# First attention of an fp32 two-block model: another order for heads 0-3 and heads 4-7 around the projection blocks

## What is computed

```python
def probs(qb, k):
    s = jnp.einsum("bhqd,bhkd->bhqk", qb, k).astype(jnp.float32) * scale + bias
    return jax.nn.softmax(jnp.where(causal, s, -jnp.inf), axis=-1)
a = probs(qb1, k1) - lam * probs(qb2, k2)
out = jnp.einsum("bhqk,bhkv->bhqv", a.astype(v.dtype), v)
...
of = of * lax.rsqrt(jnp.mean(jnp.square(of), -1, keepdims=True) + LN_EPS) * subln_g
of = of * (1.0 - lambda_init)
return of.reshape(bsz, seq, V_WIDTH) @ w_o
```

## Time and profile before

| | us |
|---|---|
| median of three runs (1342.65 to 2119.0) | 1343.82 |
| profiled execution | 1342.31 |
| its span, first to last instruction | 1340.6 |

### The profile page before, as it was taken

How to read it: one execution, slowest core, us unless ns; L and a number is a source line. 1 busy time by engine, 2 the same in 40 slices (tenths; PEclk the granted TensorE clock), 3 DMA queues, 4 the chain that set the end, 5 groups by cost and what they waited for, 6 DMA issues and landing times.

```text
span 1340.6 us, 15674 instructions
## 1 busy us (share of the span) xinstructions
PE 1248.6 (93%) x6428; PEld 858.3 (64%) x6428; DVE 622.3 (46%) x944; ACT 451.7 (34%) x698; POOL 199.0 (15%) x174
## 2 busy tenths in 40 slices
PE   7998989999988996889999998989999898899998
PEld 7986654444537884654444536879887546778776
DVE  3996422221216565522221216594489644444544
ACT  3596311111113455311111113465466213444432
POOL 5000300000000000200000000185788130000000
PEclk9999989999999997989999998999999899999999
DMA  9800959999994530589999992533344133363450
GB/s 336 295 0 10 413 240 428 427 427 428 428 393 162 189 126 0 226 332 429 427 427 429 426 384 98 186 126 126 126 159 156 63 126 128 126 237 138 180 196 32
DMA packets 68162, 321.22 MB, mean 240 GB/s; under 512 B 4072, under 2 KB 12661, under 8 KB 55419
## 3 DMA queue, kind: packets, MB, share of 16 engines
q1 hardware_dynamic: 64944, 308.57, 58.1%
q0 software_dynamic: 2592, 11.42, 2.4%
q10 hardware_dynamic: 554, 0.23, 0.1%
HBM read 317.02 MB, written 3.18 MB: 239 GB/s over the span
## 4 chain that ended last, share of the span: by engine, by line
PE 75%; DVE 15%; ACT 4%; issue 3%; POOL 2%; DMA 0%; DVEq 0%; ACTq 0%; POOLq 0%
PE bank L1477 29%; PE bank L1638 25%; PE bank L1630 5%; PE bank L1542 3%; PE bank L2090 3%; PE bank L1680 2%; DVE w_lo L646 2%; ACT w_hi L934 1%; DVE arena L2217 1%; POOL w_lo L646 1%; POOL xtok L870 1%; DVE rows L2731 1%; DVE arena L2750 1%; PE bank L1761 1%; POOL xtok L868 1%
## 5 line engine op out<-in xcount | busy, mean ns | idle before, releaser
L934 ACT ACTIVATE w_hi<-ring 128x2048 fp32r<-128x2048 f32 (+1 forms) x96 | 180.1, 1880 | 213.8 <-PE bank L1477 208.2
L646 DVE TENSOR_TENSOR w_lo<-ring,w_hi 128x2048 fp32r<-128x2048 f32 (+1 forms) x70 | 156.6, 2240 | 182.6 <-ACT w_hi L934 182.1
L646 POOL TENSOR_TENSOR w_lo<-ring,w_hi 128x512 fp32r<-128x512 f32 x104 | 152.0, 1494 | 84.9 <-ACT w_hi L934 84.9
L1477 PE MATMUL bank<-w_hi,x_hi 128*128 128x512 f32 (+1 forms) x432 | 121.7, 401 | 18.0 <-ACT arena L1397 6.5
L1477 PE MATMUL bank<-w_lo,x_hi 128*128 128x512 f32 (+1 forms) x432 | 118.8, 395 | 3.7 <-POOL w_lo L646 3.4
L1477 PE MATMUL bank<-w_hi,x_lo 128*128 128x512 f32 (+1 forms) x432 | 118.3, 394 | 0.0
L1638 PE MATMUL bank<-ring,moe_x 128*64 128x512 f32 x384 | 113.0, 594 | 1.5 <-issue 1.5
L1638 PE MATMUL bank<-arena,moe_x 128*64 128x512 f32 x384 | 112.9, 594 | 0.0
L1477 PEld LDWEIGHTS bank<-w_hi,x_hi 128*128 128x128 f32 x432 | 79.5, 194 | 36.4 <-issue 11.8
L1477 PEld LDWEIGHTS bank<-w_lo,x_hi 128*128 128x128 f32 x432 | 81.8, 194 | 23.3 <-POOL w_lo L646 6.4
L2390 DVE TENSOR_TENSOR y_r<-bank,y_r 128x512 fp32r<-128x512 f32 x32 | 22.1, 692 | 158.7 <-ACT y_r L934 158.7
(11 more groups left out here) (330 smaller groups left out, 1863.1 us busy)
## 6 DMA issues: line engine op xcount, KB each, us to landing
ring<-in_w_in_dram SPq DMA_DIRECT2D x15, 2048.0 KB, 8.0
ring<-in_moe_w_gate_dram SPq DMA_DIRECT2D x12, 2048.0 KB, 16.3
arena<-in_moe_w_down_dram SPq DMA_DIRECT2D x12, 2048.0 KB, 20.6
arena<-in_moe_w_gate_dram SPq DMA_DIRECT2D x12, 2048.0 KB, 15.9
ring<-in_moe_w_down_dram SPq DMA_DIRECT2D x12, 2048.0 KB, 18.0
ring<-in_moe_w_up_dram SPq DMA_DIRECT2D x12, 2048.0 KB, 16.1
arena<-in_moe_w_up_dram SPq DMA_DIRECT2D x12, 2048.0 KB, 19.2
wslots<-in_moe_w_up_dram SPq DMA_DIRECT2D x8, 2048.0 KB, 20.6
```

The lines of the kernel that those rows point to most:

```text
L646: last = ops.tensor_tensor(part(w_lo, label, hb)[:, x].bitcast(F32R), ring_half(label, hb)[:, x], part(w_hi, label, hb)[:, x], ALU.subtract)
L934: return s.activation(dst, src, ACT.Copy)
L1477: last = mm(bank(use_)[:, at:at + cols], still, moving, start=start and opens and (hb, n, k) == (0, 0, 0), stop=stop and closes and (hb, n ...
```

## The change

- Heads 0-3: all of their units (0 to 7) now lie inside v0, k1 and q1, two steps to a unit; their norm, transposes and split lie inside v1. The split result goes to a buffer of its own, `o_hi` and `o_lo` (`o_r`, at 14336 of the arena), since `x_hi` and `x_lo` are still read by v1.
- Heads 4-7: units 8 to 11 begin inside v1, the rest inside wo0 and wo1. The lone stretch between v1 and wo0 is gone; a short one (two calls) is between wo0 and wo1.
- The last unit's sum (15) goes into a bank of its own (`o15`, bank 6) and is scaled by its own instruction (`last_head_out`), so that the other three heads can be scaled earlier.
- In the lists of ScalarE and VectorE, `weights(u)` is no longer tied to `weights_T(u - 2)`, and `logits` and `difference` are written out singly.

The diff, indentation cut; left out are changes of signatures and calls that follow from the new buffer.

```diff
@@ -131,6 +131,9 @@
+O_AT = 7 * KD * T
+with nc.sbuf_tensor("below_o", [P, O_AT], F32), nc.sbuf_tensor("o_r", [P, 2, 4, T], F32) as o_r:
+    pass
...
     use(("pT", u), 6)
     if h % 4 == 0:
         use(("o", qt, h // 4), 7)
+use("o15", 6)
 for b in range(4):
     use(("oT", b), (0, 1, 4, 5)[b])
...
-def head_squares(qt, g):
+def head_squares(qt, g, heads):
     freed(act, ("o", qt, g))
-    for h in range(4):
...
@@ -1203,50 +1208,66 @@
 keys_out("k", kT, 0)
 highs(("v", 0))
 keys_out("q", qT, 0)
+weights(0)
 high(("k", 1), 0)
-weights(0)
 weights(1)
+weights_T(0)
+values_out(0)
 high(("k", 1), 1)
-values_out(0)
-weights_T(0)
 weights_T(1)
+weights(2)
+weights(3)
+weights_T(2)
 high(("q", 1), 0)
-weights_T(2)
+weights(4)
+weights_T(3)
+weights(5)
+weights_T(4)
+high(("q", 1), 1)
+weights_T(5)
 keys_out("k", kT, 1)
-high(("q", 1), 1)
-weights_T(3)
-weights_T(4)
-head_squares(0, 0)
+weights(6)
+head_squares(0, 0, range(4))
+weights(7)
+weights_T(6)
 high(("v", 1), 0)
-weights_T(5)
+weights_T(7)
+high(("v", 1), 1)
 keys_out("q", qT, 1)
-high(("v", 1), 1)
-weights_T(6)
-weights_T(7)
+head_squares(1, 0, range(4))
+head_roots(0)
+weights(8)
+weights(9)
+values_out(1)
+for b in range(2):
+    heads_high(b, o_hi, slice(2 * b, 2 * b + 2), slice(0, T))
 weights_T(8)
-head_squares(1, 0)
-head_roots(0)
-values_out(1)
+weights(10)
 high(("wo", 0), 0)
 weights_T(9)
+weights(11)
+weights_T(10)
 high(("wo", 0), 1)
-weights_T(10)
-for b in range(2):
-    heads_high(b, slice(2 * b, 2 * b + 2), slice(0, T))
 weights_T(11)
+weights(12)
+weights(13)
+head_squares(0, 1, range(4))
 weights_T(12)
+high(("wo", 1), 0)
+weights(14)
 weights_T(13)
+weights(15)
 root_ahead()
-head_squares(0, 1)
 tile_root(0)
 weights_T(14)
-high(("wo", 1), 0)
+high(("wo", 1), 1)
+heads_high(2, x_hi, slice(4, 8), slice(0, P))
 weights_T(15)
-heads_high(2, slice(4, 8), slice(0, P))
-high(("wo", 1), 1)
-head_squares(1, 1)
+head_squares(1, 1, range(3))
+freed(act, "o15")
+head_squares(1, 1, (3,))
 tile_root(1)
-heads_high(3, slice(4, 8), slice(P, T))
+heads_high(3, x_hi, slice(4, 8), slice(P, T))
 root_ahead()
@@ -1772,14 +1793,16 @@
 def weighted(u):
     qt, h = units[u]
-    o = ("o", qt, h // 4)
-    if h % 4 == 0:
+    o, at = ("o", qt, h // 4), h % 4 * VD
+    if u == len(units) - 1:
+        o, at = "o15", 0
+    if h % 4 == 0 or o == "o15":
         claim(pe, o)
     freed(pe, ("pT", u))
     for kt in range(qt + 1):
-        last = mm(bank(o)[:, h % 4 * VD:(h % 4 + 1) * VD], diffT[:, u % 2, kt, :],
+        last = mm(bank(o)[:, at:at + VD], diffT[:, u % 2, kt, :],
                   vtok[:, kt, h * VD:(h + 1) * VD], start=kt == 0, stop=kt == qt)
-    if h % 4 == 3:
...
@@ -1799,6 +1822,8 @@
         scores(0)
     elif (hb, t) == (1, 0):
         scores(1)
+    elif (hb, t) == (1, 1):
+        weights_T(0)
 keys("k", 0, arrives="ln1")
 keys("q", 0)
@@ -1806,55 +1831,43 @@
 def during_k(hb, n):
     if (hb, n) == (0, 0):
         scores(2)
-        weights_T(0)
     elif (hb, n) == (0, 1):
         evacuated(("v", 0))
         weighted(0)
+        weights_T(1)
+    elif (hb, n) == (0, 2):
+        scores(3)
+        weighted(1)
     elif (hb, n) == (0, 3):
-        scores(3)
-        weights_T(1)
+        weights_T(2)
     elif (hb, n) == (1, 0):
-        weighted(1)
+        scores(4)
+        weighted(2)
     elif (hb, n) == (1, 1):
-        scores(4)
-        weights_T(2)
+        weights_T(3)
     elif (hb, n) == (1, 2):
-        weighted(2)
+        scores(5)
+        weighted(3)
+    elif (hb, n) == (1, 3):
+        weights_T(4)
 def during_q(hb, n):
     if (hb, n) == (0, 0):
-        scores(5)
-        weights_T(3)
+        scores(6)
+        weighted(4)
     elif (hb, n) == (0, 1):
-        weighted(3)
+        weights_T(5)
+    elif (hb, n) == (0, 2):
+        scores(7)
+        weighted(5)
     elif (hb, n) == (0, 3):
-        scores(6)
-        weights_T(4)
+        weights_T(6)
     elif (hb, n) == (1, 0):
-        weighted(4)
+        weighted(6)
     elif (hb, n) == (1, 1):
-        scores(7)
-        weights_T(5)
+        weights_T(7)
     elif (hb, n) == (1, 2):
-        weighted(5)
-def during_v(hb, t):
-    if (t, hb) == (0, 0):
-        weights_T(6)
-    elif (t, hb) == (0, 1):
-        weighted(6)
-        evacuated(("k", 1), ("q", 1))
-        scores(8)
-    elif (t, hb) == (1, 0):
-        scores(9)
-        weights_T(7)
-    elif (t, hb) == (1, 1):
         weighted(7)
-        scores(10)
-        weights_T(8)
-keys("k", 1, steps=during_k)
-keys("q", 1, steps=during_q)
-linear_tok(("v", 1), ("v", 1), steps=during_v, order=[(hb, t) for t in range(NT) for hb in range(2)])
 def heads_T(b, chunks, ts):
-def unit(u):
-    if u + 2 < len(units):
-        scores(u + 2)
-    weights_T(u)
-def out_heads(g, **more):
+def during_v(hb, t):
+    if (t, hb) == (0, 1):
+        evacuated(("k", 1), ("q", 1))
+        scores(8)
+        scores(9)
+    elif (t, hb) == (1, 0):
+        pe.wait_ge(sem("onorm"), NT)
+        for b in range(2):
+            heads_T(b, (2 * b, 2 * b + 1), range(NT))
+        scores(10)
+        weights_T(8)
+    elif (t, hb) == (1, 1):
+        freed(pe, ("v", 1, 0))
+        weighted(8)
+        weights_T(9)
+        scores(11)
+keys("k", 1, steps=during_k)
+keys("q", 1, steps=during_q)
+linear_tok(("v", 1), ("v", 1), steps=during_v, order=[(hb, t) for t in range(NT) for hb in range(2)])
+def out_heads(g, xh, xl, **more):
     split_product(("wo", g), [(("wo", t, h), HALF, slice(t * P, (t + 1) * P), slice(h * HALF, (h + 1) * HALF))
                               for t in range(NT) for h in range(2)],
-                  True, x_hi[:, 4 * g:4 * g + 4, :], x_lo[:, 4 * g:4 * g + 4, :], start=not g, stop=bool(g),
-                  **more)
+                  True, xh, xl, start=not g, stop=bool(g), **more)
 def during_wo(hb, n):
     if (hb, n) == (0, 0):
+        weights_T(10)
+        weighted(9)
         for b in range(2):
             freed(pe, ("oT", b))
     elif (hb, n) == (0, 1):
+        weighted(10)
+        weights_T(11)
+        scores(12)
+    elif (hb, n) == (0, 2):
+        freed(pe, ("v", 1, 1))
         weighted(11)
-        unit(12)
-    elif (hb, n) == (0, 2):
+        scores(13)
+    elif (hb, n) == (1, 0):
+        weights_T(12)
+        scores(14)
+    elif (hb, n) == (1, 1):
         weighted(12)
-        unit(13)
-    elif (hb, n) == (0, 3):
+        weights_T(13)
+        scores(15)
+    elif (hb, n) == (1, 2):
         weighted(13)
-        unit(14)
-    elif (hb, n) == (1, 0):
-        weighted(14)
-        unit(15)
-    elif (hb, n) == (1, 1):
-        pe.wait_ge(sem("onorm"), NT + 1)
-        heads_T(2, range(4, 8), (0,))
-        weighted(15)
+    elif (hb, n) == (1, 3):
+        weights_T(14)
 def during_wo1(hb, n):
     if (n, hb) == (0, 0):
         freed(pe, ("oT", 2))
+    elif (n, hb) == (1, 0):
+        weights_T(15)
+    elif (n, hb) == (0, 1):
+        weighted(15)
     elif (n, hb) == (2, 0):
         pe.wait_ge(sem("onorm"), 2 * NT)
         heads_T(3, range(4, 8), (1,))
         freed(pe, ("oT", 3))
-freed(pe, ("v", 1, 0))
-weighted(8)
-unit(9)
-weighted(9)
-unit(10)
-freed(pe, ("v", 1, 1))
-pe.wait_ge(sem("onorm"), NT)
-for b in range(2):
-    heads_T(b, (2 * b, 2 * b + 1), range(NT))
-weighted(10)
-unit(11)
-out_heads(0, steps=during_wo)
-out_heads(1, steps=during_wo1, order=[(hb, 2 * t + h) for t in range(NT) for hb in range(2) for h in range(2)])
+out_heads(0, o_hi, o_lo, steps=during_wo)
+pe.wait_ge(sem("onorm"), NT + 1)
+heads_T(2, range(4, 8), (0,))
+weighted(14)
+out_heads(1, x_hi[:, 4:8, :], x_lo[:, 4:8, :], steps=during_wo1, order=[(hb, 2 * t + h) for t in range(NT) for hb in range(2) for h in range(2)])
 norm_T("ln2", before=2)
 experts(1)
...
-def pair_of(u):
-    if u + 1 < len(units):
-        logits(u + 1)
-    difference(u)
-def heads_out(qt, g):
+def heads_out(qt, g, n=4):
     ready(dve, ("o", qt, g))
-    heads = lambda x: x.rearrange("p (h d) -> p h d", h=4)
+    heads = lambda x: x.rearrange("p (h d) -> p h d", h=n)
     u0 = 8 * g + 4 * qt
-    free(v.tensor_tensor(heads(otok[:, qt, g * HALF:(g + 1) * HALF]), heads(bank(("o", qt, g))[:]),
-                         bcast(dinv[:, 0, u0:u0 + 4].unsqueeze(2), 4, VD), ALU.mult), ("o", qt, g))
+    free(v.tensor_tensor(heads(otok[:, qt, g * HALF:g * HALF + n * VD]), heads(bank(("o", qt, g))[:, 0:n * VD]),
+                         bcast(dinv[:, 0, u0:u0 + n].unsqueeze(2), n, VD), ALU.mult), ("o", qt, g))
+def last_head_out():
+    ready(dve, "o15")
+    free(v.tensor_scalar(otok[:, 1, 7 * VD:8 * VD], bank("o15")[:, 0:VD], dinv[:, 0, 15:16], None, ALU.mult),
+         "o15")
 def heads_norm(g, ts, root):
     dve.wait_ge(sem("ostd"), root)
@@ -2540,49 +2568,63 @@
 low(dve, v, ("v", 0), 1)
 dve.wait_ge(sem("bias1"), 16)
 logits(0)
+difference(0)
+logits(1)
 low(dve, v, ("k", 1), 0)
-logits(1)
-difference(0)
+difference(1)
 values_out(0)
+logits(2)
 low(dve, v, ("k", 1), 1)
-pair_of(1)
-pair_of(2)
+difference(2)
+logits(3)
```

(92 more changed lines are left out.)

1 line of the change is left out of this document (removed).

## The result

Median of the changed kernel 1329.72 us against 1342.65 us of the kernel before in the same session: ratio 0.9896, 95% interval 0.9878 to 0.9914. Timed again later: 1326.28 against 1343.17, ratio 0.9874 (0.9857 to 0.9890). Faster by 1.0 to 1.3%, which is within 2%. The first two medians are each over five executions of which one ran far longer (2348.53 and 2119.0 us), which the ratio leaves out.

The account below looks back on a forecast made before the run. TensorE was taken as the bound, losing 23.3 us to waits, low clock and drain. Work to 534.3 plus 6.9 of new waits gives 541.2 against 557.5, 16.3 less: 1327.5 on the runs' scale, said as 1328, range 1322 to 1337.

Parts of the forecast that it names:

- the walk: Layer 1 attention: the new instruction orders followed with profiled durations, giving new TensorE waits of 6.9 us in all.
- 1.6, 2.1 and 1.7 predicted: Output blocks: waits for unit 14's transposes, the second output block's first product, and the last head transposes' round trip.
- The small ones (0.2, 0.5, 0.1, 0.7): Predicted waits for unit 6's sum, the first output block's low half, unit 11 and unit 12.
- one I held to be covered by 0.3: Value block: norm of heads 0-3 ready at 494.9, asked for at 495.2, so no wait.
- 89.1 predicted: TensorE's pieces summed at full clock without waits: through at 534.3, from first scores at 445.24.
- drain and fill: 487.0 to 557.5 before: 3.7 us around some ten waits, counted as not work.
- stragglers: Second half: 1 us more wait in four places, clock falling after 520.8 to 526.9 (2 us lost): +6, 1334; chance 0.22.
- The low clock before: 507:525 before, mean clock 0.53: at most 4.9 us lost, 4.3 taken.
- 23.3 us that are not work: 487.0 to 557.5 before: 15.3 waits, 4.3 low clock, 3.7 drain and fill; the most that could be won.
- The slow rival: Key and query blocks: softmax round trip doesn't fit, each of eight units 2.29 us late, 18.3 us, 1346; chance 0.04.
- The table loads of ScalarE: Value block: 1.28 us each by the row, no unit 8 wait; the skill's 2.66 would mean about 2 us wait, 1330.
- The expert loads: Behind the stage: seven blocks move with it, 6 us cover unchanged; rival gives 10 us back, 1338, chance 0.04.

Follow-up runs that it names:

- the nine fillers: Kernel before, with nine products of an identity by the mask, result unread, put into TensorE's waits: 1341.01 us against 1343.29, stage 110.54.
- the 21: Kernel before, with 21 products of an identity by the mask, result unread, put into five TensorE waits: 1345.34 us, stage 114.9.
- the added maxima: Changed kernel with one, two or four more VectorE maxima over 512 elements ahead of each of differences 0 to 7: stages 97.3, 99.5, 110.0 us.
- the common bank: Changed kernel with unit 15's sum back in its three neighbours' bank and one scaling for all four heads: 1331.33 us, stage 99.2.
- the early norm: Early root kernel, plus heads 0-3's squares and root ahead of v1's last ScalarE build, division ahead of logits 8 and 9: 1324.39 us against 1343.29, stage 94.8.
- half of it: Kernel before with only units 0 to 7 moved as in the change and heads 0-3's norm right after: 1337.24 us, stage 108.5.
- Early root: Changed kernel, difference 14 ahead of its build; heads 4-7's query block 0 root, head transposes and split earlier: 1323.21 us against 1342.97, ratio 0.9859, stage 93.7.

## Why the prediction came out as it did

The predicted time of 1328 lies between the two medians, 1326.3 and 1329.7. Its own sum, 112.3 less 16.3, makes a stage of 96.0; it was 98.5. That the time came out all the same is partly luck: the stage starts 2.8 us earlier than before, which no term of the prediction has, and that makes up for a stage 2.5 us too long. The end of the output product at 540.96, where the prediction said 541, is the same meeting of two errors. The median fell by 12.9 us in the first session and by 16.9 in the second, so it can't tell 16.3 from 13.8.

For the stage I count waits as the walk did, by the distances between the starts of groups. Three terms were off, with both signs: 96.0 - 0.3 + 1.3 + 1.55 = 98.5 (rounded).

- **Waits: 6.9 predicted, 6.6 measured.** The reported waits are 5.35, but a report counts from the modelled end of the group before. The sums ahead of the second output block start at 522.72 and take 0.36 like those at 517.38, so TensorE stood still from 523.08 to 525.34, 2.26 us where 2.01 is reported. Counted so, the four waits are 0.68, 1.43, 2.26 and 1.74, and two that aren't reported add 0.2 (the low half, 502.91) and 0.3 (unit 12's transposes, 511.15). The large ones were right in place and nearly in size: 1.6, 2.1 and 1.7 predicted. The run with difference 14 ahead of the build shows the first's cause. The small ones (0.2, 0.5, 0.1, 0.7) came to 0.5 instead of 1.5, and one I held to be covered by 0.3 came.
- **Work at the full clock: 89.1 predicted (534.3 less 445.24), 90.3 measured** (98.49 less 6.6 and 1.55). This is the step that failed: the walk found 3.7 us of "drain and fill" in before, laid them to the waits and put them at nothing in the new order. Some 0.2 us for each of the 11 waits of before may have been just that, but the rest were pieces priced too low, and these stay. The excess lies in the output blocks: 32.0 us of work in place of 30.6. The chain's 1.40 holds for a step behind another step. With transposes, sums or scores around it a step takes up to 1.51:

```profile
515.87 1.20 PE L1498 MATMUL bank<-w_hi,o_r 128*128 128x512 f32 x4
516.91 0.63 PE L1498 MATMUL bank<-w_lo,o_r 128*128 128x512 f32 x2
517.38 0.61 PE L1803 MATMUL bank<-arena 128*128 128x128 f32 x4
```

  (515.87 to 517.38). The sixteen steps come to about 23.4 us in place of 22.4 (the last three take 1.36 each), the small transposes and sums to 3.6 in place of 3.1. The blocks before it nearly cancel: 0.3 more in the key and query blocks, 0.4 less in the value block.
- **Clock: no loss predicted, 1.55 measured.** The forecast said 1.00 in 500:520, which came, and that a stretch at the low level behind 527 would show it wrong, which came too. That was the rival "stragglers", which named the thin stretch between 520.8 and 526.9 and put the clock at up to 2 us; its other part, 1 us more of waits in four places, did not come. So half a rival was true.
- **The low clock before: 4.3 predicted, 4.0 measured** by the nine fillers (about 4.5 by the 21). With 4.0 the gain of 13.8 splits into 10.2 of reported waits, 2.4 of clock (4.0 less 1.55) and 1.2 of the rest. The last fits the unreported part of the 7 waits that went, at some 0.2 each; that is an estimate and not a run. All of it the prediction had as "23.3 us that are not work".
- **Key and query blocks.** No wait in 455:487, as said, and the added maxima show the margin: one us of VectorE per unit is free, the next isn't. The slow rival was refuted.
- **The table loads of ScalarE.** Its timeline in the kernel after:

```profile
489.19 1.28 ACT L1191 ACT_TABLE_LOAD   x1
490.49 0.30 ACT L1191 ACTIVATE small<-small,eps_ln 128x8 f32<-128x8 f32 x1
490.81 1.28 ACT L1168 ACT_TABLE_LOAD   x1
492.10 0.40 ACT L1168 ACTIVATE arena<-arena,small 128x128 f32<-128x128 f32 x1
```

  Two loads and a root take 2.91 us, 489.19 to 492.10, and each operation starts 0.01 us behind its load: the row held and unit 8 brought no wait. The Trainium skill (ScalarE: Activation LUTs, "What ACT_TABLE_LOAD costs") gives about 2.66 us for one switch, 5.3 for the two; the trace doesn't agree, and the measurement decides.
- **The expert loads** move with the stage, as said: the first gate product starts at 568.65, 27.7 us behind the end of the output product, as before. What lies behind the stage takes 783.1 us with a stage of 112.3, 783.8 with 98.5 and 783.0 with 93.7: nothing was given back. (Two profiles have more, 785.8 with the common bank and 786.7 with the early norm; I haven't traced that. The latter's profiled execution was also the longest of its runs, 1327.49.)

## What to carry to other kernels

- A stretch in which TensorE waits between two dense products costs twice: the waits, and what runs at the low clock after them (here 10.3 of the 15.6 us of waits, and about 4.0 us). Fillers won back only the second; the order that removes the stretch got most of both, and half of it only part of the first (3.8 of 13.8 us).
- In a walk the large waits came out right, and an amount for the pieces' edges must be kept: here 1.3 us in 90.3. Take a piece's price from a row with the neighbours that it will have, and count a wait from the start of the group before plus its price: the reported wait is shorter by some 0.2 us.
- An engine's idle time ahead of an instruction that waits is not free for anything: look at what stands behind it in its queue first.

## What of the hardware was not expected

- The drop of the clock isn't settled by the order of TensorE's instructions and the length of the gap. After a gap of 2.01 us it came at once in both profiles of the change, and behind 1.44 us in the one with difference 14 earlier. It did not come behind the same 2.01 with one or two VectorE maxima per unit added some 40 us and more before it; with four it came one group of products later. With unit 15 in the common bank it came behind the later gap of 1.56 in place of the 2.01. Early root, with one gap of 1.56, had none. What tells these apart stays open.
- A float32 product of an identity by 128x512 took two passes of 0.44 us.
